# A weight stream of 2 MB loads in three places instead of 1 MB loads in four, and two constants moved into dead space

## The reference, cut to what matters

```python
branches = jnp.stack([y_fox, y_lru, y_sb, y_mem], axis=2)
gates = jax.nn.sigmoid(proj("gates").reshape(b, s, N_BRANCH, D_MODEL) + b_gate[l])
projected = jnp.einsum('bsnc,ncd->bsnd', branches, w_branch[l])
mixed = jnp.sum(gates * projected, axis=2)
...
# the experts of the second block: each takes the tokens that its router column ranks highest
hid = jax.nn.silu(jnp.einsum('becd,edf->becf', xin, w1)) * jnp.einsum('becd,edf->becf', xin, w3)
ye = jnp.einsum('becf,efd->becd', hid, w2) * gate[..., None].astype(h.dtype)
```

## Time and profile before

| | |
|---|---|
| median of 3 runs | 2921.23 us (2916.26 to 2926.79) |
| the profiled execution's own time | 2923.55 us |
| its span, first to last instruction | 2921.7 us |
| mean granted clock | 0.961 |
| PE, DVE, ACT, POOL busy | 88%, 35%, 30%, 15% of the span |
| read from HBM | 666 MB |

### The profile page before, as it was taken

The page is one execution under the profiler, slowest core; times in us unless marked ns, Lnnn a source line. Parts: engine busy times, 40 slices in busy tenths (PEclk is TensorE's granted clock), DMA queues, the critical chain, the costliest instruction groups (busy, mean ns, idle before and its releaser), DMA issues. The chain is left out here.

```text
span 2921.7 us, 37919 instructions
## 1 busy us (share of the span) xinstructions
PE 2557.6 (88%) x15020; PEld 1780.0 (61%) x15020; DVE 1031.8 (35%) x1526; ACT 883.8 (30%) x1398; POOL 429.1 (15%) x217
## 2 busy tenths in 40 slices
PE   7999989999999998999977888887897987788877
PEld 7888878899997677688732222224776973222222
DVE  4547522146753534544430011114445651000001
ACT  4555533344443434322420000002335441000001
POOL 0430026670010221000310000000231020000000
PEclk8999999999999999899989999998998989999999
DMA  4434337764543111322289999995221567999996
GB/s 180 160 135 154 116 113 276 278 226 159 186 150 119 64 57 58 159 90 98 108 336 411 396 406 414 410 398 229 101 83 58 186 228 296 405 404 415 413 408 281
DMA packets 92888, 669.44 MB, mean 229 GB/s; under 512 B 10288, under 2 KB 10432, under 8 KB 12736
## 3 DMA queue, kind: packets, MB, share of 16 engines
q1 hardware_dynamic: 90256, 654.63, 57.2%
q0 software_dynamic: 2208, 11.56, 1.1%
q10 hardware_dynamic: 272, 1.05, 0.1%
HBM read 666.13 MB, written 1.06 MB: 228 GB/s over the span
## 5 line engine op out<-in xcount | busy, mean ns | idle before, releaser
L2450 PE MATMUL ps<-ring,WK 128*64 128x512 f32 x2984 | 710.5, 607 | 144.6 <-DMA ring<-in_stream 120.6
L561 PE MATMUL ps<-A,piece_hi 128*128 128x256 f32 (+1 forms) x1952 | 622.5, 319 | 35.4 <-ACTq L458 7.2
L562 PE MATMUL ps<-A,piece_hi 128*128 128x256 f32 (+1 forms) x1952 | 608.7, 312 | 0.0
L563 PE MATMUL ps<-A,ring_lo 128*128 128x256 f32 (+1 forms) x1952 | 608.1, 312 | 0.0
L2450 PEld LDWEIGHTS ps<-ring,WK 128*64 128x64 f32 x2984 | 191.6, 137 | 628.1 <-DMA ring<-in_stream 327.4
L471 ACT ACTIVATE piece_hi<-ring 128x1024 fp32r<-128x1024 f32 x378 | 391.4, 1053 | 266.5 <-DMA ring<-in_stream 120.7
L561 PEld LDWEIGHTS ps<-A,piece_hi 128*128 128x128 f32 x1952 | 380.8, 195 | 77.2 <-issue 43.4
L482 POOL TENSOR_TENSOR ring_lo<-ring,piece_hi 128x1024 fp32r<-128x1024 f32 x123 | 313.7, 2564 | 701.4 <-ACT piece_hi L471 701.4
L480 DVE TENSOR_TENSOR ring_lo<-ring,piece_hi 128x1024 fp32r<-128x1024 f32 x255 | 319.4, 1257 | 263.2 <-ACT piece_hi L471 262.6
L562 PEld LDWEIGHTS ps<-A,piece_hi 128*128 128x128 f32 x1952 | 381.3, 195 | 18.4
L563 PEld LDWEIGHTS ps<-A,ring_lo 128*128 128x128 f32 x1952 | 380.4, 195 | 18.6
(11 more groups left out here) (272 smaller groups left out, 2638.1 us busy)
## 6 DMA issues: line engine op xcount, KB each, us to landing
ring<-in_stream SPq DMA_DIRECT2D x610, 1024.0 KB, 7.5
WK<-in_ahead SPq DMA_DIRECT2D x5, 1024.0 KB, 10.4
WK<-in_na_bias POOLq DMA_DIRECT2D x2, 2048.0 KB, 7.8
hi_place<-in_ahead SPq DMA_DIRECT2D x4, 1024.0 KB, 14.1
WK<-cum_scratch POOLq DMA_DIRECT2D x1, 2048.0 KB, 9.7
A_place<-in_ahead SPq DMA_DIRECT2D x2, 1024.0 KB, 17.3
const<-in_const SPq DMA_DIRECT2D x1, 1235.0 KB, 10.2
WK<-in_x SPq DMA_DIRECT2D x1, 1024.0 KB, 4.9
```

What stands on the lines that cost most here:

```text
L561: nc.tensor.matmul(out_, l[0], r[0], start=first, stop=False)
L562: nc.tensor.matmul(out_, l[0], r[1], start=False, stop=False)
L563: return nc.tensor.matmul(out_, l[1], r[0], start=False, stop=last)
L2450: last = nc.tensor.matmul(ps[64 * n:64 * n + 64, bank, :], lhs, piece[:, n * 512:n * 512 + 512], start=(k == 0), stop=(k == DC - 1))
```

## The change

- A load is now 2 MB: four pieces, rows of 16 KB in each partition. The ring has three places of 2 MB, twelve pieces. Piece p lies in place `p // 4 % 3`.
- SP waits for the fourth piece of a load (`piece_used[3]`) before its place is filled again.
- The loads ahead stand behind the load of pieces 384 to 387 in layer 0 and behind the load of pieces 852 to 855 in layer 1.
- The ring needs 16 KB more in each partition. To make room, `const` now lies under a second name `const_r` of type float32r. The unit matrix and the mask of the stick-breaking attention are rounded in place of `causal` and of `sb_mask` itself (`sb_eye`, `sb_mask`), and `ROWS` lies over `causal` and a part of `sb_mask`. `sb_const` and the tensor `ROWS` are gone.
- The projection up of the feed-forward network, a hardware loop of two turns of four tiles, is now written out, since its 16 pieces are no multiple of the twelve in the ring.
- In `split_ahead` the bound `cur.p + 2 * R - 2` grows from 6 to 10 pieces with `R` = 6.

```diff
-R = 4
+R = 6
+PLACES = R // 2
...
+            const = place.enter_context(nc.sbuf_tensor("const", [P, N_CONST], F32))
...
+        const_r = ctx.enter_context(nc.sbuf_tensor("const_r", [P, N_CONST], F32R))
...
-        ROWS = sb("ROWS", [P, 512])
...
+        sb_eye = const_r[:, CONSTS["causal"][0]:CONSTS["causal"][0] + P]
+        sb_mask = const_r[:, CONSTS["sb_mask"][0]:CONSTS["sb_mask"][1]]
+        ROWS = const[:, CONSTS["causal"][0]:CONSTS["causal"][0] + 512]
...
-            act.wait_ge(landed[slot], cur.piece_use(cur.s, 1, 16, 2 * R))
+            act.wait_ge(landed[slot // 2], cur.piece_use(cur.s, 1, 16, 2 * R))
...
-            with loop(eng, cur, 2, pieces=16, banks=16, steps=steps, steps_per=4 * per) as i:
-                for j in range(4):
-                    tile_(i * 4 + j)
-            for j in range(8, UPS):
+            for j in range(UPS):
                 tile_(j)
...
-                sp.dma_start(ring[:, j, :], a["stream"][one(t)].rearrange("a p w -> (a p) w")).then_inc(landed[j], 16)
+                sp.dma_start(ring[:, 2 * j:2 * j + 2, :].rearrange("p a w -> p (a w)"),
+                             a["stream"][one(t)].rearrange("a p w -> (a p) w")).then_inc(landed[j], 16)
...
-                turns = (end - t) // R
+                turns = (end - t) // PLACES
                 with sp.Fori(0, turns) as i:
-                    for j in range(R):
-                        q = 2 * j + 1
-                        sp.wait_ge(piece_used[q % 4], i * 2 + (q // 4 + 1 + (t // R - 1) * 2))
-                        load(i * R + (t + j), j)
...
+                    for j in range(PLACES):
+                        sp.wait_ge(piece_used[3], i * PLACES + (t + j - PLACES + 1))
+                        load(i * PLACES + (t + j), (t + j) % PLACES)
...
-            run(R, EXPERTS_AT[0] // 2 - 4)
+            run(PLACES, EXPERTS_AT[0] // 4 - 2)
             come_ahead(0)
-            run(EXPERTS_AT[0] // 2 - 4, EXPERTS_AT[1] // 2 + 4)
+            run(EXPERTS_AT[0] // 4 - 2, EXPERTS_AT[1] // 4 + 2)
             come_ahead(1)
-            run(EXPERTS_AT[1] // 2 + 4, N_SLOTS)
+            run(EXPERTS_AT[1] // 4 + 2, N_LOADS)
```

More of the change, by code:

```diff
@@ L16 @@
-from contextlib import ExitStack, contextmanager
+import math
+from contextlib import ExitStack
 import numpy as np
@@ L102 @@
     - sum(AHEAD_NO) * WORDS
-N_SLOTS = STREAM_WORDS // WORDS
+N_LOADS = -(-STREAM_WORDS // (2 * WORDS))
 assert STREAM_WORDS % WORDS == 0
@@ L277, in build @@
         A = ctx.enter_context(nc.sbuf_tensor("A", [P, 2, DC, 2 * T], F32R))
+        const_r = ctx.enter_context(nc.sbuf_tensor("const_r", [P, N_CONST], F32R))
         AH, AL = A[:, 0], A[:, 1]
         XT = sb("XT", [P, DC, 2 * T])
-        const = sb("const", [P, N_CONST])
         par = sb("par", [P, N_PAR])
@@ L290, in build @@
         hvar = sb("hvar", [P, 4, 16])
-        sb_const = ctx.enter_context(nc.sbuf_tensor("sb_const", [P, P + SB], F32R))
         ps = ctx.enter_context(nc.psum_tensor("ps", [P, 8, 512], F32))
@@ L320, in f32 @@
             return x.bitcast(F32)
-        landed = [sem(f"landed{s}") for s in range(R)]
+        landed = [sem(f"landed{s}") for s in range(PLACES)]
         hi_done = [sem(f"hi_done{j}") for j in range(4)]
@@ L428, in __call__ @@
                 self.eng.wait_ge(self.sem, self.n if self.i is None else self.n + self.i * self.per)
[L430 to L448, removed]
         ahead_of = []
@@ L525, in raw_piece @@
             assert RAW[cur.p]
-            pe.wait_ge(landed[slot], 16 * (cur.p // (2 * R) + 1))
+            pe.wait_ge(landed[slot // 2], 16 * (cur.p // (2 * R) + 1))
             cur.p += 1
@@ L1488, in sb_pe @@
         def sb_pe(pe, cur):
-            mask, eye = sb_const[:, P:], sb_const[:, 0:P]
             def scores(r):
@@ L1493, in scores @@
                 for a in range(2):
-                    nc.tensor.matmul(z_ps[r % 2][:, a, :], eye, mask, start=True, stop=False)
+                    nc.tensor.matmul(z_ps[r % 2][:, a, :], sb_eye, sb_mask, start=True, stop=False)
                 for qt, cols, nk in ((1, slice(0, T), T), (0, slice(T + 1, SB - 1), P)):
@@ L1561, in sb_dve @@
             flat = lambda x: x.rearrange("p a k -> p (a k)")
-            nc.vector.tensor_copy(sb_const[:, 0:P], ident)
-            nc.vector.tensor_copy(sb_const[:, P:], cst("sb_mask")).then_inc(sb_ready, 1)
+            nc.vector.tensor_copy(sb_eye, ident)
+            nc.vector.tensor_copy(sb_mask, cst("sb_mask")).then_inc(sb_ready, 1)
             for r in range(2):
@@ L2632, in _ @@
             sp.dma_start(const[:, P:], a["const"][:, P:]).then_inc(const_load, 16)
-            for j in range(R):
+            for j in range(PLACES):
                 load(j, j)
[L2635 to L2638, removed]
             def run(t, end):
-                while t % R:
-                    one_load(t)
-                    t += 1
-                turns = (end - t) // R
+                turns = (end - t) // PLACES
                 with sp.Fori(0, turns) as i:
-                    for j in range(R):
-                        q = 2 * j + 1
-                        sp.wait_ge(piece_used[q % 4], i * 2 + (q // 4 + 1 + (t // R - 1) * 2))
-                        load(i * R + (t + j), j)
-                for u in range(t + turns * R, end):
-                    one_load(u)
+                    for j in range(PLACES):
+                        sp.wait_ge(piece_used[3], i * PLACES + (t + j - PLACES + 1))
+                        load(i * PLACES + (t + j), (t + j) % PLACES)
+                for u in range(t + turns * PLACES, end):
+                    sp.wait_ge(piece_used[3], u - PLACES + 1)
+                    load(u, u % PLACES)
             def come_ahead(layer):
@@ L3121, in _stream @@
     assert sum(w.shape[1] for w in parts) == STREAM_WORDS, (sum(w.shape[1] for w in parts), STREAM_WORDS)
-    stream = np.zeros((N_SLOTS, P, WORDS), np.float32)
+    load = 2 * WORDS
+    stream = np.zeros((N_LOADS, P, load), np.float32)
     at = 0
@@ L3125, in _stream @@
         while w.shape[1]:
-            n = min(WORDS - at % WORDS, w.shape[1])
-            stream[at // WORDS, :, at % WORDS:at % WORDS + n] = w[:, :n]
+            n = min(load - at % load, w.shape[1])
+            stream[at // load, :, at % load:at % load + n] = w[:, :n]
             at, w = at + n, w[:, n:]
```

## The result

The changed kernel takes 2890.64 us (median of 4 runs, 2884.38 to 2894.32) against 2924.01 us before (4 runs on the same chip): ratio 0.9882, 95% interval 0.9858 to 0.9905, so 33 us or 1.2% faster. The prediction was 2901 us with a range from 2883 to 2914. The profiled execution is the fastest of the four: 2884.38 us, span 2882.5 us, 39.2 us under the span of before.

A forecast was written before the change was run, and what follows sets the result against it. The prediction took the DMA stream to bound two expert stretches, some 946 us, and PE to set the time elsewhere. Its terms, -7.6 - 8 - 4 - 2.5 + 1.9 = -20.2 us, gave 2901 us, range 2883 to 2914.

The forecast's parts named there:

- The rate of the full stream: Expert stages of both layers: 16 KB packets make the same bytes cost 0.8% less, -7.6 us of 946.
- rival 2: Full stream in the expert stages: the rate gains the whole 2.6%, -24.6 us there, 2884 us in all; chance 0.12.
- rival 4: Expert stages: coarse releases lengthen PE's waits, its clock falls and the DMA engines run dry, 2943 us; chance 0.07.
- estimate from the Trainium skill's ceiling of 435 GB/s: Expert stages: by that ceiling they could shrink by 3% at most, 28 us.
- Rival 1: Expert stages: the rate stays, as rows travel in two packets or cost goes by bytes alone; 2909 us, chance 0.22.
- The merge: First block, pieces 88 to 183: earlier loads remove most of PE's waits for POOL's low parts, -8 us.
- The routing: Layer 0: loads ahead go out at least 5 us earlier, shortening PE's wait for ring pieces, -4 us.
- The ring's content when the experts begin: Start of both expert stages: ten expert pieces in the ring against eight; -2.5 us in layer 1, 0 in layer 0.
- the tail: End of the expert stream: PE has four pieces to work through after the last landing in place of two, +1.9 us.
- The edits at nothing: Written-out projection up, casts, copy to `ROWS`, first load and ADA pieces from 306 on: no cost or gain, 0 us.
- The slower rival: Same as rival 4: expert stages slowed by coarse releases and PE's clock falling to 1.2 GHz, 2943 us; chance 0.07.
- a sign of being wrong: Expert stages: a granted clock under 0.98 was one of three observations named as making the prediction wrong.

The follow-up runs named there:

- the two repeats: The changed kernel, unaltered, timed twice more beside the kernel before: 2897.13 us (ratio 0.9912) and 2900.08 us (0.9926).
- the last kernel: The changed kernel with every matmul of `add_group_pe` in layer 1 done twice: 2891.76 us, ratio 0.9902 against the kernel before.
- the one with rows of 8 KB: The changed kernel with each 2 MB place filled by two 1 MB transfers with rows of 8 KB: 2899.76 us, ratio 0.9922 against the kernel before.

## Why the prediction was right, and what its sum missed

**The rate of the full stream** (-7.6 us) is the term that was mis-sized, and its reason covers only a part. By the rates, 406 to 413 GB/s is -8 us in layer 0 and 410 to 422 is -13 in layer 1; the stages are 6.9 and 12.8 us shorter, some -20 together, where rate, ring content and tail had made -8.2. In layer 1 about two thirds of it come with rows of 8 KB already, from the ring alone. I took the DMA share of 1.00 for a full queue, so that only the cost of a packet could lift the rate. But the share also counts a packet as busy while it takes longer than usual: by the records of single packets, those above 1.5 times the usual 309 ns cost each engine 11.8 us more from 1530 to 2000 us before, with 6.6 us idle; with six places it is 0.4 us and none from 1510 to 1940 us. The clues were in the text: rival 2's peaks of 424 against a mean of 406 to 410, and the beat itself, since 1 MB in 2.49 us is already 421 GB/s. Six places of 1 MB hold 421 with the same packets. A third clue stood in rival 4: what is still in flight when a place is released, (places - 1) times the time of a load, less the time that PE reads one. I worked it out as 5.5 us before and 6.0 after, and took both for enough. The experiments, with the same formula:

| ring | in flight at release | time | rates of the two layers |
|---|---|---|---|
| 2 places of 2 MB | 1.1 us | 3470 us | 280, 304 |
| 4 of 1 MB (before) | 5.5 | 2921 to 2923 | 406, 410 |
| 3 of 2 MB (changed) | 6.0 | 2891 to 2900 | 413, 422 |
| the same, borders moved | 6.0 | 2878 | 423, 422 |
| 5 of 1 MB | 8.0 | 2876 | 421, 421 |
| 4 of 1.5 MB | 8.3 | 2874 | 425, 426 |
| 6 of 1 MB | 10.5 | 2871 | 421, 421 |

The formula orders the rings only roughly: the two rows with 6.0 us differ by 10 GB/s in layer 0. It leaves out PE's gap of 2.3 us behind the 16th piece and its 1 to 2 us of `add_group_pe`; by the same sum about 4 us are left in flight where the first falls into a load (an estimate). From 8 us on only the size of the packet still raises the rate. The Trainium skill ("DMA: Bandwidth & Descriptors", Anatomy of one DMA — SWDGE (gpsimd) path) gives a transfer issued by GpSimd a fixed cost of about 2.0 us and lays most of it to the confirmation at its end. The prediction, which took the figure with the section on bandwidth, had it that three transfers in flight hide such a cost already. No run shows the cost itself; 421 GB/s with five places against 406 to 410 with four says that with four the queue was not kept full. The prediction's estimate from the Trainium skill's ceiling of 435 GB/s is wrong as a sum: 3% is the way from the beat's 421, and from the stages' own 406 and 410 it would be 6%, some 59 us. It also counted slices 21 and 34 among the full ones, where the share is 8 and 7 tenths.

**The packets.** The changed kernel has 46,336 packets on its queue, about half, as named:

```profile
q1 hardware_dynamic: 46336, 654.61, 57.1%
```

What they are worth with a full queue stands in the beat. In layer 1 of the changed kernel sixteen matmuls follow each other every 4.89 us (2753.19 to 2758.08 us above), 2 MB at 429 GB/s, against 1 MB in 2.49 us, 421 GB/s, in the earlier trace rows: some 1.7% from 8 to 16 KB, twice the 0.8% that I took, beside 1% from 8 to 12 KB. The stages get less of it, as their queue isn't always full (413 and 422 GB/s, 422 to 425 with moved borders). Rival 1 (rows travel in two packets) falls with the count. Rival 2's 2884 us is 7 us from the first time, but 13 and 16 from the two repeats, farther than the forecast's 2901, and its reason holds in part: a 2.6% cheaper byte was not reached, and the depth of the queue freed room too.

**The merge** (-8 us, measured -9.2) went as put there: no wait of PE for POOL is left, and PE is busy for 177.00 of 177 us. It asks for a deeper ring, not for larger loads: five places of 1 MB give 177.6 us. The part of the working that counted on loads aligned with SPLIT and ADA pairs isn't needed; with moved borders it is 179.1 us, also without a wait for POOL. ACT's waits for landings sank, over 425 to 602 us of the changed kernel:

```profile
ACT piece_hi L455 <- DMA ring<-in_stream: 73.9, 22, 6.3
```

**The routing** (-4 us, measured -7.0) was right in sign for a reason that falls. PE and SP in order of time in the changed kernel:

```profile
1461.88 0.47 PE L558 MATMUL ps<-const,WK 64*128 64x64 f32 x2 [4.92 <-DVE WK L2386]
...
1475.58 1.06 PE L1941 MATMUL ps<-ring,CS 128*32 128x512 f32 x8 [2.96 <-DMA ring<-in_stream]
...
1452.62 0.90 SPq L2631 DMA_DIRECT2D WK<-in_ahead  x2
```

The loads ahead go out well before 1469 us, and the wait of 8.12 us is down to 2.96. But moving them earlier alone gives nothing (60.3 us), and five places of 1 MB give 54.7. The ring's twelve pieces alone don't give it either. With moved borders the ring holds as many and the loads ahead go out at 1449.07 us, and the stage takes 60.1 us:

```profile
1473.41 1.93 PE L1942 MATMUL ps<-ring,CS 128*32 128x512 f32 x8 [5.01 <-DMA ring<-in_stream]
1475.28 3.78 PE L561 MATMUL ps<-WKR,A 128*128 128x512 f32 x8
```

What goes with the length is the piece that follows the loads ahead: 60.3 and 60.1 us at piece 386, with eight and with twelve pieces in the ring (in both PE waits one slot sooner, 5.60 and 5.01 us, and the eight matmuls behind take 3.74 and 3.78 us in place of 2.11); 56.6 at piece 387; 53.1 to 57.8 at piece 388, in seven profiles of five kernels with ten or twelve; 59.9 and 60.5 at piece 390 with eight. Only two places of 2 MB break the row (66.7 at piece 388), where every stage is longer. A kernel with the old ring and piece 388 was not run, so the cause stays open, and that the term came out near its -4 is luck. The stage varies, too: 53.5, 53.1 and 57.8 us in three executions of the changed kernel.

**The ring's content when the experts begin** (-2.5 us in layer 1) and **the tail** (+1.9) can't be read apart. PE reads ten pieces ahead of its first wait, as named, but before it had read twelve, since at the low clock there a refill kept up. The rate accounts for the whole of layer 1's 12.8 us, so the two together came to about nothing, where I had -0.6.

**The edits at nothing** are confirmed, at 1.0006 (0.9991 to 1.0021).

**Missed** was a cost: the stretch before the merge is 4.1 us longer. Waits of PE and issues in the whole changed kernel:

```profile
PE ps L560 <- DMA WK<-in_lru_w: 6.6, 1, 6.6
```

```profile
WK<-in_lru_w POOLq DMA_DIRECT2D x1, 1024.0 KB, 9.4
```

This load goes out on POOL's queue beside those of the ring, and PE waits for it. It takes 6.9 us to land and PE waits 4.1 us before, so 2.5 of the 4.1 us come from it. The size of the neighbouring transfers isn't the cause: with pairs of 1 MB it takes 9.3 us, with 2 MB loads at moved borders 5.2, and with six places of 1 MB 6.8. So the moment may decide; it was not tried apart.

**The slower rival** did not come true in the first profile: PE waits 1.23 to 1.25 us in one piece at a granted clock of 0.99 and 1.00. But its clock shows in two other profiles, both of executions of 2904 us. In the last kernel and in the one with rows of 8 KB, layer 0's experts run at a mean granted clock of 0.98 and 0.97 and take 482.1 and 481.7 us; in the first, 40 us of them run at 0.87 and 382 GB/s. The second of these is under the 0.98 that the prediction named as a sign of being wrong. Two places of 2 MB show it in full.

**Luck.** Besides the routing, the 4.1 us that were missed before the merge stand against a rate term that was too small by some 11 us, and the two repeats gained 26 and 23 us, nearer to the forecast's 20 than the first 33.

**Open.** Why layer 0 of the changed kernel varies from 472.1 to 476.3 us from one execution to the next while layer 1 stays within 457.8 to 459.7 (the 482.1 us go with a lower clock, but what made PE wait first isn't shown); what made the routing shorter; and why a gap in the middle of a load costs layer 1 nothing at 1.13 us of `add_group_pe`.

## What to carry to other kernels

For a ring that refills a saturated queue, work out what is in flight at the moment when a place is released, with the reader's own gaps in it: (places - 1) x time of a load - time from landing to release. Here rings with 8 us or more held the full rate of their packets, and those with 5.5 and 6.0 us mostly did not. The sum is a guide and no law: with the same three places, moving the borders of the loads, so that the reader's longer gaps fell elsewhere, won 22 us. Try more and finer places before making transfers larger: 6 MB as six loads of 1 MB beat three of 2 MB by 26 us, and one more place of 1 MB won 45 us. And read a DMA share of 1.00 together with the peaks of the rate and the shortest beat; where the mean is under what the same packets reach at their best, the queue runs low.

## What the runs showed of the hardware

- Once the queue is full, the rate goes with the row: 421 GB/s with packets of 8 KB, 425 to 426 with 12 KB, 429 in the beat of 2 MB in 4.89 us with 16 KB.
- A DMA share of 1.00 stood beside 406, 410, 416 and 422 GB/s, and 1.01 beside 421 with packets of 8 KB and 426 with packets of 12 KB: the share doesn't tell a full queue from a nearly full one.
- Where PE reads a 2 MB load, the place of the borders against PE's two gaps in an expert is worth 10 to 15 us of layer 0's stage (472.1, 475.2 and 476.3 us in three executions, against 461.7 and about 461).
- Two places of 2 MB are far too few: the rate is 280 and 304 GB/s, and the granted clock of the stretches 0.80 and 0.86, beside waits of nearly 5 us.
- A single wait of 2.58 us at full clock was followed by eight matmuls in 2.89 us in place of 1.94, and a granted clock of 0.87 over 40 us.
